# Loads of the retention states: begun by the sync engine behind the weights, not by ScalarE

## The reference

```python
def step(s, inp):                       # here one position: c = 1
    qc, kc, vc = inp
    ...
    s = g_c[None, :, None, None] * s + jnp.einsum('bmhk,bmhv->bhkv', kc * zeta[None, :, :, None], vc)
    return s, o

mp, sp = retention_mixer(hp, s0, w_in_ret[j], w_out_ret[j])              # prompt
ms, ss = retention_mixer(hs, state_ret[j], w_in_ret[j], w_out_ret[j])    # 8 samples
```

## Time and profile before

| what | value |
|---|---|
| median of 3 runs | 1932.83 us (1932.66 to 1934.03) |
| the profiled execution: time | 1937.19 us |
| its span, first to last instruction | 1935.4 us |
| mean granted TensorE clock | 0.966 of full speed |
| TensorE busy | 1849.3 us, 96% of the span |
| DMA | 346.33 MB, mean 179 GB/s |

### The profile page before, as it was taken

One profiled execution on the slowest core, in us unless ns is written; L12 is line 12 of the kernel. 1 busy time (PEld: TensorE's weight loads), 2 busy tenths in 40 slices (PEclk: granted clock), 3 DMA queues, 4 the chain that ended last, 5 costly groups with the idle time before them and its releaser, 6 DMA issues.

```text
span 1935.4 us, 32448 instructions
## 1 busy us (share of the span) xinstructions
PE 1849.3 (96%) x14116; PEld 1781.6 (92%) x14116; DVE 1042.3 (54%) x1119; ACT 911.4 (47%) x1064; POOL 778.8 (40%) x226
## 2 busy tenths in 40 slices
PE   8999989999979999999999979999999999899997
PEld 7999989999879999989989969999999999899997
DVE  5455554764487745354545452776354545647753
ACT  5556555343553344353434433544455555553333
POOL 5455435554224443412211200345455545355541
PEclk9999989999989999999999977999999999899999
DMA  8766855555335555844545521355667678545552
GB/s 266 251 227 245 290 176 172 175 174 180 104 109 177 182 184 167 244 149 134 162 135 154 143 69 43 127 184 164 189 229 238 231 252 294 184 143 175 174 180 83
DMA packets 306036, 346.33 MB, mean 179 GB/s; under 512 B 7847, under 2 KB 269479, under 8 KB 305887
## 3 DMA queue, kind: packets, MB, share of 16 engines
q1 hardware_dynamic: 257968, 260.36, 42.9%
q10 hardware_dynamic: 47927, 83.90, 12.6%
HBM read 299.66 MB, written 44.82 MB: 178 GB/s over the span
## 4 chain that ended last, share of the span: by engine, by line
PE 81%; DVE 9%; ACT 4%; issue 3%; DMA 2%; ACTq 1%; PEldq 0%; DVEq 0%
PE acc L1476 20%; PE acc L1477 20%; PE acc L1483 20%; PE mix L1914 2%; PE mix L1616 2%; PE mix L1875 1%; PE mix L1538 1%; DMA out_dram<-st 1%; PE acc L1504 1%; PE mix L1847 1%; ACT w_hi L428 1%; PE acc L1505 1%; PE acc L1510 1%; PE mix L1628 1%; DVE st L1029 1%
## 5 line engine op out<-in xcount | busy, mean ns | idle before, releaser
L1383 POOL TENSOR_TENSOR w_lo<-raw,w_hi 128x2048 fp32r<-128x2048 f32 (+2 forms) x163 | 695.1, 4268 | 728.6 <-ACT w_hi L428 728.6
L1476 PE MATMUL acc<-g_hi,w_hi 128*128 128x264 f32 x2576 | 658.0, 293 | 9.5 <-DVE gate L1172 3.2
L1477 PE MATMUL acc<-g_lo,w_hi 128*128 128x264 f32 x2576 | 646.8, 288 | 0.0
L428 ACT ACTIVATE w_hi<-raw 128x2048 fp32r<-128x2048 f32 (+3 forms) x260 | 455.9, 1755 | 166.7 <-PE acc L1483 78.3
L917 DVE TENSOR_TENSOR w_lo<-raw,w_hi 128x2048 fp32r<-128x2048 f32 (+1 forms) x97 | 376.2, 3878 | 270.4 <-ACT w_hi L428 270.4
L1476 PEld LDWEIGHTS acc<-g_hi,w_hi 128*128 128x128 f32 x2576 | 493.5, 192 | 18.5 <-issue 13.0
L1477 PEld LDWEIGHTS acc<-g_lo,w_hi 128*128 128x128 f32 x2576 | 496.4, 193 | 1.2
L1483 PE MATMUL acc<-g_hi,w_lo 128*128 128x264 f32 x2576 | 351.1, 287 | 0.0
L1483 PEld LDWEIGHTS acc<-g_hi,w_lo 128*128 128x128 f32 x2576 | 333.9, 190 | 1.5
L1416 POOL TENSOR_TENSOR h_lo<-hid,h_hi 128x528 fp32r<-128x528 f32 x44 | 59.2, 1344 | 333.5 <-ACT h_hi L702 333.5
L1476 PE MATMUL acc<-h_hi,w_hi 128*128 128x264 f32 x664 | 164.1, 284 | 0.0
(11 more groups left out here) (232 smaller groups left out, 2427.2 us busy)
## 6 DMA issues: line engine op xcount, KB each, us to landing
raw<-in_w_ffn_in_dram SPq DMA_DIRECT2D x88, 1024.0 KB, 5.3
raw<-in_w_in_ret_dram SPq DMA_DIRECT2D x48, 1024.0 KB, 6.8
raw<-in_w_in_attn_dram SPq DMA_DIRECT2D x36, 1024.0 KB, 5.5
st<-in_state_ret_dram ACTq DMA_DIRECT2D x64, 512.0 KB, 6.6
out_dram<-st ACTq DMA_DIRECT2D x64, 512.0 KB, 6.0
raw<-in_w_ffn_out_dram SPq DMA_DIRECT2D x32, 768.0 KB, 4.9
raw<-in_w_ffn_out_dram SPq DMA_DIRECT2D x32, 640.0 KB, 5.1
raw<-in_w_out_ret_dram SPq DMA_DIRECT2D x16, 1024.0 KB, 6.9
```

The costliest lines, as they stand in the source:

```text
L428: A(w_hi[:, u % SPL, 0:size[u]], raw[:, u % RAW, 0:size[u]], ACT.Copy).then_inc(hi_split, 1)
L1383: TT(w_lo[:, u % SPL, 0:size[u]], raw[:, u % RAW, 0:size[u]], w_hi[:, u % SPL, 0:size[u]].bitcast(F32), ALU.subtract).then_inc(lo_by_pool, 1)
L1476: MM(out, wh, x_hi[:, ks[k], :], start=first and k == 0, stop=False)
L1477: MM(out, wh, x_lo[:, ks[k], :], start=False, stop=False)
```

## The change

The loads leave ScalarE's stream and go into SP's, on the queue that carries the weights. After the load of each unit of a retention layer SP issues the loads that ScalarE issued in the same step, with the same two waits: five behind unit 2, two each behind units 9, 10, 11, then behind 14 to 17 and 20 to 23 and 26, and three behind unit 27. In layer 3 the first five are issued behind its unit 2 also, and wait only for the end of the attention layer, whose buffers lie in the same place. Everything else in ScalarE's stream keeps its order, and VectorE, GpSimd and TensorE keep theirs.

```diff
+            def states_to(r, end):
+                for n in range(sent[r], min(end, 32)):
+                    g = 32 * r + n
+                    if g == 32:
+                        sp.wait_ge(std_ready, 2 * ATT_SUB + 2)
+                    if g >= ST:
+                        sp.wait_ge(st_stored[g % ST], 16 * (g // ST))
+                        sp.wait_ge(t_ready, g - ST + 1)
+                    sp.dma_start(st[:, g % ST], state_view(r, n)).then_inc(st_landed[g % ST], 16)
+                    sent[r] = n + 1
+            def states_behind(u):
+                for r, sub in enumerate(ret_subs):
+                    at = u - where[sub, "in"] - 2
+                    if at == 0:
+                        states_to(r, ST)
+                    elif 6 <= at < 24:
+                        states_to(r, 8 * (at // 6 - 1) + 2 * min(at % 6, 3) + ST)
+                    elif 24 <= at < 28:
+                        states_to(r, 24 + 4 * (at - 24) + ST)
...
                 sp.dma_start(raw[:, u % RAW, 0:k * UC].rearrange("p (k n) -> p k n", k=k), units[u])\
                     .then_inc(raw_landed[u % RAW], 16)
+                states_behind(u)
...
-                def load_to(end):
...
-                load_to(ST)
...
-                        if h:
-                            load_to(n + 4)
                         if h or s:
                             hi(ub + s + 2)
                         if h:
                             t_first(n)
                             store(n)
-                            load_to(n + 5)
                             scale_to(n + 3)
...
                     scale_to(n + 2)
-                    load_to(n + 4)
```

More of the change, by code:

```diff
@@ L389, in cache_part, with state_view @@
                 sp.dma_start(buf[64:80, :, 1, :], v2).then_inc(landed, 16)
+            sent = [0, 0]
+            def state_view(r, n):
+                return state_ret[r, n % 8, n // 8].rearrange("(k p) v -> p k v", p=P)
+            def states_to(r, end):
[17 more added lines that the diff above has]
+                        states_to(r, 24 + 4 * (at - 24) + ST)
             sp.dma_start(x_rows[:, :, 0:D // 2], x_half[:, :, 0:D // 2]).then_inc(in_x, 16)
@@ L603, in ret_mixer @@
                     if h:
-                        load_to(8 * h + 4)
                         gn_square(h - 1)
@@ L617, in ret_mixer @@
                     hi(ub + 7)
-                    if h:
-                        load_to(8 * h + 5)
                     act.wait_ge(s0_done, gh + 1)
```

## The result

| what | before | after |
|---|---|---|
| median | 1933.43 us (4 runs, 1932.66 to 1934.49) | 1966.12 us (4 runs, 1951.39 to 1976.28) |
| the profiled execution: time | 1937.19 us | 1951.39 us |
| its span | 1935.4 us | 1949.6 us |
| TensorE busy | 1849.3 us | 1847.6 us |

The ratio is 1.0163, with an interval of 1.0095 to 1.0231. The changed kernel is 32.7 us slower. My forecast was 1932.3 us with a range up to 1942, so it was wrong. The rival "weights come late" names the right place and mechanism; the measured time lies beyond even its end of 1950.

The account below looks back on a forecast made before the run. TensorE, busy 96% of the span, was taken as the bound, ScalarE's waits as nearly all covered. Unit 17's +0.8 and the tail's -1.4 gave -0.6 us, about 1932.3 us on the median; range 1925 to 1942.

Parts of the forecast that it names:

- weights come late: Slower rival: units 16, 17 and likes delayed in SP's queue behind two store waits; 1942 to 1945 us, chance 0.30.
- the term of unit 17: Loaded heads: unit 17, behind the store of state 11, lands 0.3 us late; +0.4 us a layer, +0.8 on both.
- Unit 16, "Cost 0": Head 2: `hi` of unit 16 begins as now; head 3: 1 to 2 us late with 2.6 to spare; cost 0.
- The bound: High end for unit 17: store keeps 8 us, unit takes 10.5, lands 5.0 late; six heads give +30.
- The rival's price: Late weights: unit 17 landing 1.5 to 2 us later than the sum costs six heads 9 to 12 us.
- Unit 18, "Cost 0": Head 2: unit 18 lands near 163, but TensorE needs it only at the start of head 3; cost 0.
- The tail and the starts: Tail: state 30 loads 3.4 us earlier, gain 0.7 us a layer, -1.4; starts: first five states load earlier, 0.
- The clock in the tail: Faster rival: less waiting keeps the granted clock up in the tails; 1922 us at the lowest, 1927 in one layer; chance 0.18.
- the signs I had named: Changed profile: `hi` waits for units about as long as for stores before (12.1 us); state 30's scaling waits for no DMA.
- The one that was to show me wrong: Heads: TensorE's waits for `tq` growing by more than 1 us in a head would mean the weights are late.
- The rule weighed in the prediction: SP's queue: descriptors go in order, so units cannot overtake states; without it +0.8 would be -0.6, the sum -2.0 us.

Follow-up runs that it names:

- Experiment 6: The changed kernel with the loads of states 13 and 14, and like pairs, moved from behind unit 15 to behind unit 16; ratio 1.0041, median 1937.69 us.
- experiment 9: The kernel before, unchanged, profiled a second time; 1920.58 us.
- experiment 10: The changed kernel, unchanged, profiled a second time; 1963.31 us.
- experiment 7: The changed kernel with the loads of states 15 and 16, and like pairs, moved from behind unit 16 to behind unit 17; ratio 1.0051, median 1942.8 us.
- experiment 1: The changed kernel with SP keeping each wait at its place, but ScalarE issuing the state loads as in the kernel before; ratio 1.017.
- experiment 2: The changed kernel with each pair of state loads, and its waits, one unit later in SP's stream; ratio 1.0004, median 1932.65 us.

## Why the prediction was wrong

**The step that failed** is the term of unit 17, in the sentence "they share ScalarE's queue with the loads now and will have it alone, so I take 5.3". The store of state 11 is issued 16.7 us after the start of head 2 in both kernels (139.68 before, 143.73 after). It took 7.7 us to land, and 8.0 before. After:

```profile
L562 ACTq DMA_DIRECT2D out_dram<-st x1: 378/378/378, 143.7 to 143.7; - x1
...
DMA to landing us min/median/max: 7.7/7.7/7.7
```

Before:

```profile
L543 ACTq DMA_DIRECT2D out_dram<-st x1: 378/378/378, 139.7 to 139.7; - x1
...
DMA to landing us min/median/max: 8.0/8.0/8.0
```

In heads 1 and 3 of the changed kernel its like took 7.5 and 8.8, in the second layer 7.9, 8.8 and 7.9; before, these five took 5.1 to 7.1. Having ScalarE's queue alone did not help: the other queue holds two states and unit 16 at that time. My own sum had unit 16 in flight from 136.8 to 144.5, right over this store, and I still priced the store near a quiet one. The store of state 10, issued at 140.1, before unit 16 was, landed in 3.3. Experiment 6 is the counter-proof: with unit 16 loaded earlier the same store takes the 5.3 us I had assumed, and unit 17 is not late; over all six heads this store takes 4.2 to 6.2 us there, and unit 17 or its like is at most 2.0 us late. So the two waits are a chain that the sum had cut: the wait ahead of 16 moves its transfer onto the store that unit 17 waits for. The rest of the term was good. From the issue of unit 17 to its landing I had 8.5 us, measured were 7.4.

**Unit 16, "Cost 0"**, was short too: 1.1 us in head 2 (its store took 3.7 us, not 3.1, and the unit 8.9), but 3.3 in head 3, where I gave 1 to 2 and trusted 2.6 us of reserve. (It was not loaded "long before head 2 began" in the kernel before: it was issued at 118.4 and landed at 123.6, 0.6 us after the start of the head, but 22 us ahead of its `hi`.) By the starts of `hi` from the start of the head, before and after, unit 17 and its likes are late by 4.0, 2.1, 4.4 us in the first layer and 4.7, 4.5, 2.1 in the second. I had 0.3.

**The bound** of that term, 5.0 us late in six heads for +30, was taken from the slowest rows. The lateness of 2.1 to 4.7 us lies inside it; the +31.1 us of the heads lie just outside, since the bound had no term for the clock. I put the value near the low end with an argument and not with a row. Half way between its ends, the forecast would have been on the right side.

**The rival's price** of 9 to 12 us was too small twice over: it took 1.5 to 2 us beyond the sum's 0.3 where the lateness was 2.1 to 4.7, and it had no term for the clock. I used the clock for the tail and forgot it in the heads, where 14.7 of 31.1 us are the clock's.

**Unit 18, "Cost 0"**, nearly held: its `hi` begins 5 to 7 us later than before in every head, but TensorE's waits at the start of the following head are 0.4 and 0.2 us, those of before. But ScalarE has the norm's square (`gsq`) right behind this `hi`: in head 3 of the second layer `hi` stood 5.41 us for its unit, and TensorE then waited 0.45 us for `gsq`. In the heads before it waits nowhere for that, and 0.12 us once in experiment 9.

**The tail and the starts.** The scaling of state 30 waits for no DMA any more, as said. TensorE's waits of 1.27 and 1.38 us became 0.50 and 1.37 in the first layer:

```profile
278.72 0.50 PE L1618 MATMUL mix<-v_stack,sel 128*128 128x512 f32 x1 [0.50 <-DVE st L1040]
281.56 1.05 PE L1627 MATMUL mix<-tbase,tq 128*128 128x1 f32 x8 [1.37 <-DVE tq L1049]
285.93 1.05 PE L1627 MATMUL mix<-tbase,tq 128*128 128x1 f32 x8 [0.52 <-DVE tq L1049]
```

So the 0.7 us that the sum took off this wait are gone, and 0.52 us of waiting for the next `tq` are new. In the whole it can't be seen. The stretches from the last head to the next norm were 86.6 and 88.1 us, and 90.5 and 88.1 in experiment 10; before had 89.2 and 88.9, and 87.5 and 89.8 in experiment 9. The means differ by 0.5 us, one kernel's own by up to 3.9, so the gain is not shown. The start up to the first head took 64.5 and 66.4 us, before 65.6 and 64.5: no gain there that can be told from the spread.

**The clock in the tail**, the faster rival: the mean granted clock from the last head to the next norm was 0.94 and 0.94 before, 0.98 and 0.96 after, but 0.96 and 0.92 in experiment 9 and 0.91 and 0.96 in experiment 10. It differs as much between two executions of one kernel, so the rival is not shown either.

Of the signs I had named, the exchange of the store's wait for one on units came true, but not "about as long" (12.1 against 30.8 us). The one that was to show me wrong came: more than 1 us of waiting for `tq` in a head.

**The rule weighed in the prediction.** In experiment 7 two units issued 0.6 us apart land at 145.6 and 148.6, 3.0 us apart: one after the other, about the 2.8 us that 1.05 MB take at 369 GB/s. In the profile of the changed kernel states and units alike land in the order of their issue on SP's queue, all 342 transfers. With this the trace agrees with the Trainium skill's "DMA: Bandwidth & Descriptors" (queues, rings and completion order), by which a queue's descriptors are taken in order, though a later one may finish its write first; among these transfers none landed first. So the sum was right to put the states ahead of unit 17. It was not what decided: experiment 1 has no states in SP's queue and loses as much.

**What stays open.** Why the clock in the attention layer differs between executions of one kernel. Whether a kernel gains from loads on SP with waits placed by need: one unit later was the same as before, and no place tried was faster.

## What to carry to other kernels

A prefetch queue must not wait for anything that the consumer of the prefetched data comes just ahead of: put the wait behind the last transfer that is needed soon (in experiment 2, one unit later), or keep it in the stream of an engine that has time. When a wait moves ahead of a transfer, follow that transfer into the time where it now runs and ask whose landing it delays, above all the one that the next wait is for. And where TensorE's clock was at 1.00 throughout, give a new wait of more than about 1 us a term for the clock too: here 16.4 us of new idle time came with 14.7 us of slower products.

## What the runs showed of the hardware

In the profile of the changed kernel a store of 512 KB landed in 2.8 to 5.7 us when no unit was in flight on SP's queue as it was issued (37 stores, 20 of them within 3.7 us), and in 6.3 to 8.8 us when one was (27 stores); a queue of its own did not shield it. The clock went with TensorE's longest wait. In the twelve profiles, 72 loaded heads, the mean granted clock was 1.00 in 55 of the 56 heads where that wait was at most 1.03 us (and 0.97 in one). Of the 16 heads with a longer one, 1.10 to 5.13 us, 14 had a mean of 0.92 to 0.97 and two, with 1.14 and 1.15 us, had 1.00. The length alone does not set the cost: 1.90 us came with 0.92, and 4.14 us with 0.97. The stretch of attention, the same in all of them, took 443.2 to 459.0 us over twelve profiles. Two executions of the kernel before alone are 15.7 us apart in it, so a single profile of this kernel can't measure a change of that size by its total; the lengths of its parts can.
